# A router that works on the rows ahead of the first norm, with the norm running beside it and one routing chain for both token blocks

## What is computed

```python
x = layer_norm(DEEPNORM_ALPHA * x + mix, ln1_g[l], ln1_b[l])
ffn = moe_ffn(x, router_w[l], router_b[l], w_gate_up[l], b_gate_up[l], w_down[l], b_down[l])
x = layer_norm(DEEPNORM_ALPHA * x + ffn, ln2_g[l], ln2_b[l])
...
# layer_norm: (xf - mu) * rsqrt(var + LN_EPS) * g + b, over the 1024 features of a token
# moe_ffn:
logits = (xt @ router_w + router_b).astype(F32)
top_logit, top_e = lax.top_k(logits, TOP_K)
top_w = jax.nn.softmax(top_logit, axis=-1)
...
# each expert: gate/up product (1024 x 2048), clipped gated activation, down product (1024 x 1024),
# weighted with top_w and summed over the token's four experts
```

## Time and profile before

| | us |
|---|---|
| median of 3 runs | 1135.6 |
| the runs | 1129.99, 1135.60, 1135.62 |
| span of the profiled execution | 1131.7 |
| PE busy in it | 1062.0 (94%) |
| DVE, ACT, POOL busy | 239.4, 151.1, 20.5 |
| read from HBM | 425.04 MB, 376 GB/s over the span |

### The profile page before, as it was taken

One profiled execution on the slowest core, in us unless ns is written; L12 is line 12 of the kernel. 1 busy time (PEld: TensorE's weight loads), 2 busy tenths in 40 slices (PEclk: granted clock), 3 DMA queues, 4 the chain that ended last, 5 costly groups with the idle time before them and its releaser, 6 DMA issues.

```text
span 1131.7 us, 14828 instructions
## 1 busy us (share of the span) xinstructions
PE 1062.0 (94%) x5442; PEld 463.3 (41%) x5443; DVE 239.4 (21%) x734; ACT 151.1 (13%) x316; POOL 20.5 (2%) x49
## 2 busy tenths in 40 slices
PE   7999999989999999999999989999999999999895
PEld 6777644333534333333232323434333334343331
DVE  3354663201111111110111101111111111111014
ACT  2043611010101010100010100101010101010020
POOL 2000210000000000000000000000000000000000
PEclk9999999989999999999999989999999999999999
DMA  9723459969999999999999999999999999999993
GB/s 312 268 112 76 189 203 385 403 271 396 426 425 426 426 426 426 426 426 426 426 426 424 427 395 428 427 426 427 429 426 426 426 422 426 426 425 426 426 427 131
DMA packets 49412, 426.45 MB, mean 377 GB/s; under 512 B 5114, under 2 KB 9003, under 8 KB 16587
## 3 DMA queue, kind: packets, MB, share of 16 engines
q1 hardware_dynamic: 48666, 425.37, 90.9%
q10 hardware_dynamic: 720, 0.74, 0.2%
HBM read 425.04 MB, written 1.05 MB: 376 GB/s over the span
## 4 chain that ended last, share of the span: by engine, by line
PE 63%; DMA 33%; DVE 2%; issue 1%; ACT 1%; SPq 0%; DVEq 0%
PE PB L789 60%; DMA WB<-in_w_down_dram 29%; DMA WB<-in_w_gate_up_dram 3%; PE PB L1164 1%; DMA X<-in_x_dram 0%; PE PB L796 0%; DVE S L1569 0%; PE PB L893 0%; DVE S L1825 0%; DVE S L1603 0%; DVE K L1816 0%; DVE X L1608 0%; PE PB L894 0%; PE PB L895 0%; DVE K L1586 0%
## 5 line engine op out<-in xcount | busy, mean ns | idle before, releaser
L789 PE MATMUL PB<-WB,S 128*64 128x512 f32 (+5 forms) x3456 | 757.5, 593 | 40.0 <-DMA WB<-in_w_down_dram 30.9
L789 PEld LDWEIGHTS PB<-WB,S 128*64 128x64 f32 (+2 forms) x3456 | 258.7, 139 | 517.4 <-issue 438.7
L1702 DVE TENSOR_SCALAR S<-PB 128x512 f32<-128x512 f32 (+1 forms) x34 | 23.5, 691 | 482.8 <-PE PB L789 482.8
L789 PE MATMUL PB<-S 32*64 32x512 f32 (+5 forms) x456 | 104.5, 588 | 1.5 <-ACT S L710 1.4
L714 ACT ACTIVATE S<-S 128x512 f32<-128x512 f32 x32 | 20.2, 630 | 471.8 <-DVE S L1702 471.8
L1744 DVE COPY S<-PB 64x512 f32<-64x512 f32 x31 | 21.2, 684 | 281.0 <-PE PB L789 281.0
L789 PEld LDWEIGHTS PB<-S,X 128*128 128x128 f32 x512 | 59.7, 192 | 12.6 <-issue 12.2
L789 PE MATMUL PB<-S,X 128*128 128x128 f32 x512 | 63.9, 278 | 0.1
L789 PE MATMUL PB<-S,WB 128*128 128x256 f32 (+2 forms) x336 | 60.1, 377 | 0.4 <-ACT S L548 0.4
L789 PEld LDWEIGHTS PB<-S 32*64 32x64 f32 (+5 forms) x456 | 30.9, 147 | 62.9 <-issue 58.8
L730 ACT ACTIVATE S<-PB 64x512 f32<-64x512 f32 x31 | 18.4, 593 | 249.1 <-PE PB L789 249.1
(11 more groups left out here) (214 smaller groups left out, 332.5 us busy)
## 6 DMA issues: line engine op xcount, KB each, us to landing
WB<-in_w_gate_up_dram SPq DMA_DIRECT2D x128, 2048.0 KB, 25.8
WB<-in_w_down_dram SPq DMA_DIRECT2D x128, 1024.0 KB, 21.9
WB<-in_w_in_dram SPq DMA_DIRECT2D x3, 2048.0 KB, 15.3
WB<-in_w_in_dram SPq DMA_DIRECT2D x1, 2144.0 KB, 10.3
WB<-in_w_in_dram SPq DMA_DIRECT2D x2, 1024.0 KB, 10.6
WB<-in_w_out_dram SPq DMA_DIRECT2D x2, 1024.0 KB, 10.3
WB<-in_w_out_dram SPq DMA_DIRECT2D x1, 2048.0 KB, 7.9
WB<-in_w_in_dram SPq DMA_DIRECT2D x1, 1040.0 KB, 12.2
```

The lines of the kernel that those rows point to most:

```text
L789: return mm_(o, l, r, start=start, stop=stop, skip_group_check=True)
L1702: ts(g, gate, LIMIT, None, ALU.min).then_inc(s[g_ok], 1)
```

## The change

- **Router without the norm.** With m the mean and r the reciprocal deviation of a token's row y, and W the router's weights, the logits of the normed row are r * (y @ (g*W)) - r * m * (sum of g*W) + (sum of b*W) + bias. PE now transposes y itself instead of the normed rows, ahead of the norm, and multiplies with `rwg` = g*W. The two sums over the features are made once, and DVE puts the pieces together for each token (`logit_rest`, then one instruction per block with r).
- **Weights with g.** Two new small loads bring g and b as columns (`gcol`, `bcol8`: eight features on each partition, in pieces of 16 bytes), issued by SP behind `w_in`; the load of `rw` moves ahead of those of `lng` and `lnb`. POOL multiplies `rw` by g and by b and adds up over eight feature groups, six instructions that stand ahead of its first L521. One product on PE after `out_project(1)` sums over the partitions, and DVE copies the result and adds the bias to it after `add_mixed(1)`.
- **Norm in three parts.** DVE writes (y - mean) * g straight into x_sb (`centred`), ACT scales by 1/deviation (`scale_rows`), and POOL adds b (two instructions for each block, semaphore `x1ok`). The second DVE pass of each block is gone. `gather` now waits for `x1ok`, which the transposes no longer do.
- **One chain.** The two blocks' logits lie side by side; the search for the four largest is one chain with wider instructions, `route` is bumped once, and PE makes all five count products after it.
- **Start.** PE runs ten 128x128 products of `ident` with itself before it waits for x.

The router's part of the diff and the rest that is spoken of below:

```diff
+            for t, src in ((gcol, ln1_g), (bcol8, ln1_b)):
+                sp.dma_start(t.rearrange("p (h m) -> p h m", h=2),
+                             src[0].rearrange("(h p m) -> p h m", p=P, h=2)).then_inc(s["rw_ld"], 16)
...
+            sp.dma_start(rw.rearrange("p (h m) e -> p h m e", h=2),
+                         router_w[0].rearrange("(h p m) e -> p h m e", p=P, h=2)).then_inc(s["rw_ld"], 16)
             for t, src in ((lng, ln1_g), (lnb, ln1_b)):
                 sp.dma_start(t, src[0:1, :].broadcast_to([P, D])).then_inc(s["ln_ld"], 16)
-            sp.dma_start(rw.rearrange("p (h m) e -> p h m e", h=2),
-                         router_w[0].rearrange("(h p m) e -> p h m e", p=P, h=2)).then_inc(s["ln_ld"], 16)
...
+            pool.wait_ge(s["rw_ld"], 48)
+            pool.wait_ge(s["pta"], NSA)
+            pool.wait_ge(s["ptb"], NSA)
+            pool.tensor_tensor(rwg, rw, gcol.unsqueeze(2).broadcast_to([P, KT, N_EXPERTS]), ALU.mult).then_inc(s["rwg_ok"], 1)
+            pool.tensor_tensor(rwb, rw, bcol8.unsqueeze(2).broadcast_to([P, KT, N_EXPERTS]), ALU.mult).then_inc(s["rwg_ok"], 1)
+            pool.wait_ge(s["rwg_ok"], 2)
+            pool.tensor_tensor(half_sums[:, 0], rwg[:, 0:4, :], rwg[:, 4:8, :], ALU.add)
+            link(pool.tensor_tensor(half_sums[:, 1], rwb[:, 0:4, :], rwb[:, 4:8, :], ALU.add))
+            link(pool.tensor_tensor(half_sums[:, :, 0:2, :], half_sums[:, :, 0:2, :], half_sums[:, :, 2:4, :], ALU.add))
+            pool.tensor_tensor(feature_sums, half_sums[:, :, 0, :], half_sums[:, :, 1, :], ALU.add).then_inc(s["rwg_ok"], 1)
...
             for b in range(TB):
                 reciprocal_deviation(b)
+                for h in range(2):
+                    pool.wait_ge(s["x1s"], 2 * b + h + 1)
+                    xh = x_sb[:, b, 512 * h:512 * h + 512].rearrange("p (m q) -> p m q", q=P)
+                    pool.tensor_tensor(xh, xh, lnb[:, 512 * h:512 * h + 512].rearrange("p (q m) -> p m q", q=P), ALU.add)\
+                        .then_inc(s["x1ok"], 1)
...
             act.wait_ge(s["op"], 12)
             act.dma_start(bgu[0:N_EXPERTS, :], b_gu[0]).then_inc(s["bgu_ld"], 16)
             act.dma_start(bgu[32:32 + N_EXPERTS, 0:D], b_gu[0][:, D:2 * D]).then_inc(s["bgu_ld"], 16)
-            for b in range(TB):
+            def scale_rows(b):
+                act.wait_ge(s["lnp"], b + 1)
                 for h in range(2):
-                    act.wait_ge(s["x1t"], 2 * b + h + 1)
...
-            act.wait_ge(s["x1ok"], 2 * TB)
+                    act.wait_ge(s["x1n"], 2 * b + h + 1)
+                    xh = x_sb[:, b, 512 * h:512 * h + 512]
+                    act.activation(xh, xh, ACT.Copy, scale=st[:, 24 + 4 * b + 2:24 + 4 * b + 3]).then_inc(s["x1s"], 1)
+            scale_rows(0)
+            for n, (b, h) in enumerate(x1t_order):
+                act.wait_ge(s["x1t"], n + 1)
+                act.activation(x1T[:, 4 * h:4 * h + 4, P * b:P * b + P],
+                               PB[x1t_bank(b, h)][:, :].rearrange("p (k t) -> p k t", k=4), ACT.Copy)\
+                   .then_inc(s["x1tsb"], 1)
+            act.wait_ge(s["lgp"], 1)
+            act.activation(lgT[:, :, :].rearrange("p b t -> p (b t)"), PB[0][:, 0:256], ACT.Copy).then_inc(s["lgc"], 1)
+            scale_rows(1)
+            act.wait_ge(s["route"], 1)
...
+            pe.wait_ge(s["cst"], 1)
+            for _ in range(10):
+                mm(PB[7][:, 0:P], ident, ident, True, True)
             pe.wait_ge(s["x_in"], 16)
-            pe.wait_ge(s["cst"], 1)
...
+            pe.wait_ge(s["rwg_ok"], 3)
+            pe.wait_ge(s["rms_in"], 1)
+            mm(PB[0][:, 64:128], before[:, P:256], feature_sums, False, True).then_inc(s["sums"], 1)
...
-            pe.wait_ge(s["ln_ld"], 48)
             pe.wait_ge(s["foldok"], 1)
+            for b, h in x1t_order:
+                pe.wait_ge(s["ymix"], 12 if (b, h) == (1, 1) else 11)
+                for k in range(4):
+                    ins = tr(PB[x1t_bank(b, h)][:, P * k:P * k + P], every_fourth(y[:, b, 512 * h:512 * h + 512], k), ident)
+                    if k < 2:
+                        ins.then_inc(s[("xguc", "xdnc")[k]], 1)
+                ins.then_inc(s["x1t"], 1)
+            pe.wait_ge(s["sums"], 2)
+            for k in range(KT):
+                if k % 4 == 0:
+                    pe.wait_ge(s["x1tsb"], (2, 4)[k // 4] + (k == 0))
+                q = 32 * (k % 4)
+                ins = mm(PB[0][q:q + 32, 0:256], rwg[:, k, :], x1T[:, k, :], k < 4, k >= 4)
+            ins.then_inc(s["lgp"], 1)
+            stay_busy(PB[3], 1)
+            pe.wait_ge(s["lgc"], 1)
             for b in range(TB):
-                if b == 1:
...
-                mm(PB[b][:, 256:256 + N_EXPERTS], lgT[:, b, :], fold, True, True).then_inc(s["lgt"], 1)
+                ins = mm(PB[1][:, N_EXPERTS * b:N_EXPERTS * b + N_EXPERTS], lgT[:, b, :], fold, b == 0, True)
+            ins.then_inc(s["lgt"], 1)
+            stay_busy(PB[3], 5)
             pe.wait_ge(s["route"], 1)
             mm(PB[2][:, 0:32], before[:, 0:P], msk[:, 0, :], True, False)
             mm(PB[2][:, 32:64], before[:, P:256], msk[:, 0, :], False, False)
             mm(PB[2][:, 64:96], before[:, P:256], msk[:, 0, :], False, False)
-            stay_busy(PB[3], 2)
-            pe.wait_ge(s["route"], 2)
             mm(PB[2][:, 32:64], before[:, 0:P], msk[:, 1, :], False, False)
             mm(PB[2][:, 64:96], before[:, P:256], msk[:, 1, :], False, True).then_inc(s["cntp"], 1)
             stay_busy(PB[3], 2)
...
                 ins.then_inc(s["ct"], 1)
             pe.wait_ge(s["ohs"], 1)
+            pe.wait_ge(s["x1ok"], 3)
             gather(0, 6)
+            pe.wait_ge(s["x1ok"], 4)
             gather(1, 7)
...
+            dve.wait_ge(s["sums"], 1)
+            dve.wait_ge(s["smalls"], 48)
+            cp(gsum, PB[0][:, 64:96])
+            tt(bsum, PB[0][:, 96:128], rb, ALU.add).then_inc(s["sums"], 1)
+            dve.wait_ge(s["sums"], 2)
...
-            def norm(v, b, n, g, bt, dst, loaded, place=lambda a: a, view=lambda a: a):
+            def spread(b, half_first):
                 o = 24 + 4 * b
+                link(half_first)
                 link(dve.bn_aggr(st[:, o:o + 2], st[:, 12 * b:12 * b + 12]))
                 ts(st[:, o + 1:o + 2], st[:, o + 1:o + 2], LN_EPS, None, ALU.add).then_inc(s["lnstat"], 1)
-                dve.wait_ge(s[loaded], 48 if loaded == "ln_ld" else 32)
...
-                    yield stt(place(dst[:, b, c]), view(v[:, b, c]), st[:, o + 2:o + 3], view(bt[:, c]), ALU.mult, ALU.add)
+            def centred(b, h):
+                c = slice(512 * h, 512 * h + 512)
+                stt(by_rows(x_sb[:, b, c]), in_order(y[:, b, c]), st[:, 24 + 4 * b:24 + 4 * b + 1], in_order(lng[:, c]),
+                    ALU.subtract, ALU.mult).then_inc(s["x1n"], 1)
+            def logit_rest(b):
+                o = 24 + 4 * b
+                dve.wait_ge(s["lnp"], b + 1)
+                link(ts(rest[:, b, :], gsum, st[:, o:o + 1], st[:, o + 2:o + 3], ALU.mult, ALU.mult))
+                link(tt(rest[:, b, :], bsum, rest[:, b, :], ALU.subtract))
+            add_mixed(6)
+            dve.wait_ge(s["ymix"], 7)
+            link(half_stats(y, 0, 0))
+            add_mixed(7)
+            dve.wait_ge(s["ymix"], 8)
+            spread(0, half_stats(y, 0, 1))
+            dve.wait_ge(s["ln_ld"], 32)
+            centred(0, 0)
+            add_mixed(8)
+            centred(0, 1)
+            add_mixed(9)
+            logit_rest(0)
+            add_mixed(10)
+            dve.wait_ge(s["ymix"], 11)
+            link(half_stats(y, 1, 0))
+            add_mixed(11)
+            dve.wait_ge(s["ymix"], 12)
+            spread(1, half_stats(y, 1, 1))
+            centred(1, 0)
+            logit_rest(1)
+            centred(1, 1)
+            dve.wait_ge(s["lgt"], 1)
             for b in range(TB):
-                for n in ((6,), (8, 9, 10))[b]:
...
-                dve.tensor_reduce(msk[:, b, :], oh4[:, b, :, :], AX.X, ALU.add).then_inc(s["route"], 1)
+                link(stt(lg[:, b, :], PB[1][:, N_EXPERTS * b:N_EXPERTS * b + N_EXPERTS], st[:, 24 + 4 * b + 2:24 + 4 * b + 3],
+                         rest[:, b, :], ALU.mult, ALU.add))
+                ins = dve.max(m8[:, b, :], lg[:, b, :])
+            link(ins)
+            for b in range(TB):
+                ins = dve.max_index(idx8[:, 8 * b:8 * b + 8], m8[:, b, :], lg[:, b, :])
+            link(ins)
+            link(cp(idx4f.rearrange("p (b k) -> p b k", b=TB), idx8.rearrange("p (b j) -> p b j", b=TB)[:, :, 0:4]))
+            link(tt(oh4, iota_s[:, 0:N_EXPERTS].unsqueeze(1).unsqueeze(3).broadcast_to([P, TB, N_EXPERTS, 4]),
+                    idx4f.rearrange("p (b k) -> p b k", b=TB).unsqueeze(2).broadcast_to([P, TB, N_EXPERTS, 4]), ALU.is_equal))
+            dve.tensor_reduce(msk, oh4, AX.X, ALU.add).then_inc(s["route"], 1)
+            for b in range(TB):
```

(5 more changed lines are left out.)

67 lines of the change are left out of this document (15 added, 52 removed).

## The result

| | before | after |
|---|---|---|
| median | 1132.05 us (20 runs) | 1135.19 us (20 runs) |
| lowest, highest | 1129.67, 1135.62 | 1132.90, 1138.14 |
| span of the profiled execution | 1131.7 | 1132.6 |

The ratio is 1.0023, 95% interval 1.0014 to 1.0031: the change makes the kernel 2.6 us slower. It is within the 0.5% that the prediction called "the same", but the sign is clear, and it is the other sign. The 1135.19 lies 0.3 from the predicted 1134.9 by accident: I had built on a median of three runs, 1135.6, and with twenty it is 1132.05. The working has to be judged by its difference, -0.7 forecast, +2.6 measured.

The account below looks back on a forecast made before the run. PE sets the pace up to the load issued at 235.42 us, the loads after it. Router 1.1 us sooner less 0.4 for shared access gives 0.7: 1135.6 - 0.7 = 1134.9 us, range 1129.4 to 1137.9.

Parts of the forecast that it names:

- The start: Ten products ahead of x: shorter transposes, but the gain is waited off at `w_in`; 0, at most 0.2 us.
- POOL's six instructions: Weight sums ahead of the mixer's root: 3.3 us, ending at 137.9; the root slips by 0.8, PE is not delayed.
- The sums' product: One more PE product for the feature sum after the mixer: +0.25 us, last out-projection then ends at 164.7.
- Block 1's variance: DVE ahead of block 1's norm: variance ready at 167.5 us, not at 168.0.
- The chain without interference: Joint routing chain of both blocks on DVE: 2.5 us in all, against 1.59 before; mask ready at 173.9.
- What shared access costs: Four POOL additions beside DVE's strided passes and chain: 0.4 us, bounds nothing to 1.2 for each addition.
- POOL and DVE block each other: Rival, router: additions 1.8, root 171.95, mask 177.3, one-hots 179.7, 2.3 us later than before, 1137.9; chance 0.15.
- POOL began 0.8 us later: Block 0's additions on POOL: forecast to start at about 166.25, after ACT's two load issues and first scaling.
- PE's clock falls: Rival: PE waits for mask and one-hots, its clock drops, +1.7 us of PE work, 1136.6; chance 0.08.
- POOL stays off the chain: Rival: block 1's root by 168.6, logits at 170.6 start the chain, 1.85 us sooner, 1133.6 with the start; chance 0.12.
- Gain is passed on: PE's router gain reaches the end through SP's issue at 235.42; rival that it is not, 1135.6, chance 0.05.
- other level: Rival: one of three runs of before was 5.6 us lower without change; median falls there, 1129.3; chance 0.1.

Follow-up runs that it names:

- e2: Changed kernel without POOL's four additions of the norm's b (left out of the computation); 1132.33 us, ratio 0.9996 to before.
- f2: Changed kernel with ten more filler products on PE, four ahead of the logits, 11 instead of 5 behind the fold; 1140.36 us, ratio 1.0069.
- e3: Changed kernel with POOL's additions reading b in order instead of every fourth element (wrong features, same work); 1134.30 us, ratio 1.0009.
- e1: Changed kernel with POOL computing both blocks' reciprocal deviations ahead of its four additions; 1136.19 us, ratio 1.0026.
- f1: Kernel before with only the ten 128x128 start products added ahead of x; 1138.30 us, ratio 1.0061.
- g1: Kernel before with ten one-column products ahead of its first transpose, same instruction count as ten whole ones; 1137.90 us, ratio 1.0046.
- h1: Kernel before with its 11 fillers of 256 columns as 7, most of 512; 1132.06 us, ratio 0.9989.
- i1: Kernel before with ten one-column products behind the last expert's gate/up products instead of at the start; 1136.83 us, ratio 1.0050.
- f3: Changed kernel without POOL's four additions of b and without the ten start products; 1130.89 us, ratio 0.9986 to before.
- g2: Changed kernel with ten one-column products in place of its ten whole start products; 1135.15 us, ratio 1.0020 to before.
- e4: Changed kernel without the ten start products, additions still on POOL; 1132.01 us, ratio 0.9995 to before.
- f0: Changed kernel as it is, measured again beside other runs on one chip; 1134.64 us, ratio 1.0016 to before.
- h2: Changed kernel without the ten start products, b added by VectorE instead of POOL; 1131.16 us, ratio 0.9987 to before.
- j2: Changed kernel without the ten start products, b added by VectorE, ACT's two gate/up bias loads issued behind the logits' copies; 1131.12 us, ratio 0.9983.

## Why the prediction was wrong

**What held.** The start gives nothing, `w_in` absorbs it. POOL's six instructions take 2.92 us (I had 3.3), the mixer's root moved to 138.40 (137.9), and PE did not wait for it. The sums' product is 0.33 (0.25). Block 1's variance is ready at 167.49 (167.5). The chain without interference takes 171.44 to 173.89 in e2, 2.45 (2.5).

**The step that failed: "What shared access costs".** I took 0.4 us between bounds of 0 and 1.2 for each addition. It is 2.7 by the profiles of e2 and f2 and 3.1 by the ratios of e2 and the changed kernel. Three readings of the same fault: an addition was put at 1.2 by width; one that meets nothing takes that when it reads plainly (1.26 in e3), the stride adds 0.26, and two of the four waited for a strided pass and took 2.26 and 2.14. The strided pass was left at 1.10 and took 2.09. The comparison in the chain was left at 0.44 and took 1.65. I had the row that says so: L1474's 1.59 against 1.01, four instructions beside one POOL instruction, 0.6 us lost. I read it as a small loss per instruction. By the trace the first of the four took 0.87 and ended at 125.81, just behind POOL's L518 (125.72), and the other three 0.28 to 0.34, as when alone. It is one instruction held until POOL's ends, and the right question is how many POOL instructions lie beside DVE's chain, and how long each is.

The rival "POOL and DVE block each other" had this mechanism: additions 1.8 (1.86), root there at 171.95 (171.29), one held instruction in the chain at 1.2 (1.22), mask 177.3 (176.48), one-hots 179.7 (179.04), +2.3 (+2.6). It had 0.15. By the Trainium skill, GPSIMD Engine Reference, "Key points", that contention is with DVE instructions of a 2-port mode or with two SBUF inputs; the traces agree as far as they go: the strided pass, the comparison and the second instruction of logit_rest have two SBUF inputs and were held; MAX8 (0.20) and FIND_INDEX8 (0.18), with one, and L1684 (0.22), with one in PSUM, were not, beside the same additions. The cast, the first instruction of logit_rest and L1474 have one tensor input and were held too; whether they ran in a 2-port mode no view shows, and the one-column L1645, with one SBUF input as well, was not held (0.15). Who begins first matters: every DVE instruction that was held had begun after POOL's, and where the strided pass began first, POOL's addition waited. The cast took 1.20 in e1, behind the start of an addition, and 0.17 in the changed kernel, where it began at 174.16, just ahead of the last addition (174.22 by the trace). The page's rule speaks of the pairs that the change put together, and I gave it too little.

**POOL began 0.8 us later.** I let it begin at 166.25, and it began at 167.04. 0.6 of this is the last out-projection, which ended at 165.29 and not at 164.7, with the later landing. The rest is ACT's first half, which took 0.73 where I had the 0.54 to 0.63 of a copy.

**"PE's clock falls" had 0.08.** It fell between 165 and 185 in seven of thirteen profiles of kernels in the new order, and in none of five in the old (before, f1, g1, h1, i1). Without additions the router took 15.53 without the fall and 18.16 with it. PE's slow fillers then stand ahead of the counts: in f3 the counts come 2.70 us after DVE is ready for them, in e2 1.13. With the additions what a fall costs depends on where it lies. The router took 18.27 without one (f2), 18.18 and 18.24 with one that was over by 178 us (g2, e4), beside the waits for POOL, and 19.41 and 19.39 with one that went on or came behind 177 (changed, f0). So the fall costs 1.1 in the changed kernel's profile, and 2.6 in f3, where no addition covers it. The price of the additions is of the same kind: 2.7 where no fall is there (e2, f2), next to nothing where one covers them (f3, g2).

**The sum.** Forecast: router 0.7 shorter. Measured: 17.48 to 19.41, 1.9 longer: -1.95 for the idea itself (e2), +2.7 for the additions, +1.1 for the clock. With +0.4 in "last" 2.3, against 2.6 by the ratio. My -1.1 for the idea had the root as its limit; without it the rival "POOL stays off the chain" had -1.85, which is what e2 shows. The last two terms hide each other: counted in the other order it is +2.6 for the clock (f3) and +1.2 for the additions. And all of it is from single executions. Over all of them the changed kernel's mean clock is lower, 0.9893 against 0.9918, but within its own twenty the time does not follow the clock, and e4 and h2 have as low a mean (0.989) at 0.9995 and 0.9987. How the 2.6 us divide between additions and clock over all executions stays open.

**"Gain is passed on".** Held, roughly: the table's two right columns.

**The base.** Three runs gave 1135.6 where twenty give 1132.05. That, and not the reasoning, put the number near the result. The rival "other level" took for a level of its own what is spread, a part of which goes with the clock.

## What to carry to other kernels

Work moved to POOL is beside DVE's only in name: for each POOL instruction over SBUF, count on one DVE instruction on the path that waits for its end, and price it at up to POOL's length; instructions that read PSUM, MAX8 and FIND_INDEX8 were not held here. Four passes given to POOL cost 2.7 us in the profiles here, and put into DVE's own pauses 0.7 (h2 against e2). Before two profiles are compared, look at the mean clock of each and at where its execution lies among the others: two costs that hide each other, as additions and clock do here, can't be added up from single ones. And where a change adds or takes instructions on an engine with a long program, build one variant with as many instructions that do nothing before crediting the work.

## What was not expected of the hardware

Twenty more PE records ahead of 282 us (at the start in f1 and g1, as fillers in the router in f2) cost 3.6 to 4.0 us there and 2.8 to 4.1 at the end, though the tiny ones were 0.64 us of work. The number of packets on the instruction queue q8 goes from 16 to 17, of 16 KB each by the page's 0.26 MB. The Trainium skill, Advanced Engine Details and Errata, "ISA Cache", has lines of 16 KB, 256 instructions, which agrees with that. The packets can be placed in the trace: in f1, f2 and g1 one starts inside the stall near 282 (280.54, 281.66, 279.94), takes 1.07 us, and PE goes on 1.33, 1.35 and 1.26 us after its end; in the last expert of all four kernels with 5462 records PE goes on 1.7 us after one. That PE stood still for want of its own instructions is the reading that fits this, the place and the tiny products; the profile doesn't record such a wait. Why before, whose packet also lands near 282, does not stall there, stays open. The changed kernel has by chance as many records as before, 5442, so none of this is in its 2.6 us. A kernel with 20 fewer has a "last" that is 1.9 to 2.7 us shorter for it, and h2 and j2 owe part of their gain to that.
